# q and k with token parts side by side, layer norm's first steps a chunk later, and retention's output centred and gated before it is scaled

## The chip, the cores and the metric

The kernel runs on one core of a Trainium2 chip. A core has TensorE (matrix products, into PSUM), VectorE, ScalarE and GpSimd (elementwise work), and SyncE, whose queue issues the loads of the weights. Each engine runs its own list of instructions in order, and they are tied together by semaphores. The metric is the device time of one execution in microseconds (us), the median of a few runs.

## What is computed

The input is 256 tokens of 1024 channels in float32. A first block holds a gated delta rule layer and a short convolution layer; the change doesn't touch it. The second block is this:

```python
proj = h @ w_in                      # 256 x 1024 by 1024 x 11264
q, k, v, z_ret, u_val, u_gate, z_conv, g_a, g_b = jnp.split(proj, split_at, axis=-1)
qh, kh = rotary(q), rotary(k)        # 4 heads of 256 channels
ret = head_groupnorm(retention_chunkwise(qh, kh, vh))   # (o - mean) * rsqrt(var + eps), 4 heads of 512
y_a = (ret * silu(z_ret)) @ w_ret_out
a = u_val * sigmoid(u_gate)
a = causal_depthwise_conv_2(a, conv_w, conv_b)          # 31 taps over the tokens
a = silu(layernorm(a, conv_ln_g, conv_ln_b))
y_b = (a * silu(z_conv)) @ w_conv_out
merged = sigmoid(g_a) * y_a + sigmoid(g_b) * y_b
y = merged @ w_out                   # then norm, gate and residual
```

## The kernel before, in words

**Phases and chunks.** All products with weights are cut into chunks of 1 MB of weights, and the chunks into phases, in this order: qkv 16, z 8, gdn_out 8, sc_in 32, sc_out 8, glu 8, qk 8, v 8, zret 8, zconv 4, gates 8, ret_out 8, conv_out 4, w_out 4. There is no planner: the order of each engine is written out by hand, as a list of steps, one for each chunk, and what is put beside a chunk runs behind it on that engine.

**A product in three parts.** Every float32 factor is split into a high and a low part of the faster format float32r. A product is high by high, high by low and low by high. For the weights, ScalarE writes the high parts (`w_hi`, L1225) and VectorE the low ones (`w_lo = raw - w_hi`, L1795, helper `part_lo`), in halves of a chunk. In step j both make the second half of chunk j+1 and the first half of chunk j+2 (`split_hi`, `split_lo`), and then do what stands beside chunk j. `split_hi` waits until TensorE has finished the half that lay in the slot before (`half_done`), `split_lo` for `hi_ready`. TensorE waits for `hi_ready` ahead of the matmuls with `w_hi` of a half and for `lo_ready` ahead of those with `w_lo`. The load of a chunk into a ring of four slots `raw` waits for `lo_ready` of the chunk four before.

**Two forms of a chunk on TensorE.** `chunk` (L680, L681, L689) gives a half 16 matmuls of 256 columns with `w_hi`, by the high and by the low part of the tokens, and 8 with `w_lo`. `chunk_apart` (L698, L707) sends the high and the low part of the tokens, which lie side by side in `hT`, as one matmul of 512 columns, 8 for a half, and then the 8 of 256 with `w_lo`. The two parts' results then lie side by side in PSUM and must be added by someone: ScalarE copies one of them (`glu_part`), VectorE adds (`ug_sum`, `uv_sum`). sc_in and glu use `chunk_apart`, qk uses `chunk`. In a loop over a register, `chunk_apart` sends the matmuls with `w_hi` of both halves first and then those with `w_lo` of both. v, zret, gates, ret_out and conv_out go by `wide_half` (L730, L731, L737), where a half is 12 matmuls of 512 columns, those with `w_lo` last.

**VectorE beside the chunks.** The depthwise convolution is 8 channel blocks times 31 taps, 248 operations of 128x256 (`conv_op`, L2405 and L2408). `conv_share(n)` does the next n of them, and each step of glu, qk, v, zret, zconv and gates has its share. Beside qk, `rotate` multiplies a chunk in PSUM by cosine and sine (L2454, L2455) and writes `qkT` (L2457, L2458). `scores(c)` on TensorE (L1137) multiplies them behind the first four chunks of v; the first one waits for all rotations. Beside zret, TensorE does `weighted_sums` (retention's output o of head h and token tile t, in banks 4 to 7). VectorE takes its statistics (`bn_stats`, `bn_aggr` into `gmv`); ScalarE makes the square root (`grs`), VectorE the reciprocal and `gnm = -mean * grs`; ScalarE writes `og = o * grs + gnm` (L1676) from PSUM; and VectorE multiplies `og` by `zr` into `vt` (`gated`, L2490). Each head's work comes one head later; the last head's falls into zconv's first step. Behind each chunk of zconv, TensorE transposes a part of `vt` (`turn_two`, L1165), ScalarE and VectorE write it as `yT_hi`, `yT_lo` (`split_two`).

**Layer norm.** At the end of gates, VectorE adds up the convolution's channel blocks (`pair_sum`, `halves_sum`). Beside ret_out, TensorE sums over the channels by a product with ones behind chunk 1 (mean, L1174) and behind chunk 3 (variance, L1177). VectorE subtracts the mean, ScalarE squares (L1709), takes the root (L1712) and applies silu (L1716); VectorE makes the reciprocal (L2561), and the last piece is `cT_hi`, `cT_lo`, which conv_out reads.

Of the kernel before, what the change touches and what calls it, by code (L numbers as in the profile page):

```python
# [12 lines left out]
ALU = mybir.AluOpType  # L13
# [3 lines left out]
P = 128  # L17
# [82 lines left out]
def build(nc, x_in, pre_norm_w, post_norm_w, gdn_w_in, gdn_conv_w, gdn_A_log, gdn_dt_bias, gdn_norm_w, gdn_w_out,  # L100
# [3 lines left out]
    with ctx:  # L104
# [58 lines left out]
        gst, gmv, grs, gnm = new("gst", [P, NT, 6]), new("gmv", [P, NT, 2]), new("grs", [P, NT]), new("gnm", [P, NT])  # L163
# [73 lines left out]
        og = [at(f"og{t}", o_t + (9 + 2 * t) * K, [P, RDV]) for t in range(NT)]  # L237
# [344 lines left out]
        def _(pe):  # L582
# [241 lines left out]
            def wide_deep(name, a_hi, a_lo, operand, start=0, beside=None, between=None):  # L824

                g0 = FIRST[name]
                for c in range(start, COUNT[name]):
# [5 lines left out]
                    for h in range(2):  # L833
                        wide_half(g0 + c, h, c // 4 * 2, a_hi, a_lo, c % 4 * KH2, c % 4 == 0, c % 4 == 3, operand if c < 4 else None)
                    if beside is not None:
                        beside(c)

            def phase(name, a_hi, a_lo, beside=None, first=None, midway=None):
# [5 lines left out]
                def step(i):  # L844
                    for j in range(4):
# [5 lines left out]
                        elif name in ("sc_in", "glu"):  # L851
# [277 lines left out]
            def scores(c):  # L1129

                if c == 0:
                    pe.wait_ge(rp_step, 2 * RH)
# [81 lines left out]
        def _(act):  # L1214
# [425 lines left out]
            chunks("qk")  # L1640
# [25 lines left out]
            def group_norm(h):  # L1666
                act.wait_ge(gn_step, 2 * NT * (h + 1))
                if h:
                    act.wait_ge(gn_ready, NT * h)
                act.activation(grs[:, :], gmv[:, :, 1], ACT.Sqrt, bias=eps_n[:, :]).then_inc(gn_std, 1)  # L1670
                act.wait_ge(gn_rec, 2 * (h + 1))
                for t in range(NT):
                    n = NT * h + t
                    if h:
                        act.wait_ge(rg_ready, n - 1)
                    act.activation(og[t][:, :], psum[:, 4 + n % 4, :], ACT.Identity, scale=grs[:, t:t + 1], bias=gnm[:, t:t + 1]).then_inc(gn_ready, 1)  # L1676
# [26 lines left out]
            def layer_norm(i, j, done):  # L1703
                c = 4 * i + j
                if c == 1:
# [87 lines left out]
        def _(dve):  # L1793
# [622 lines left out]
            def glu_each(i, j, done):  # L2416
# [19 lines left out]
                if c >= 2:  # L2436
                    conv_share((3, 4, 5, 4, 2, 4)[c - 2])
# [12 lines left out]
            def rotate(i, j, done):  # L2450
                c = 4 * i + j
                conv_share(3)
# [210 lines left out]
```

## Time and profile before

| what | value |
|---|---|
| median of 3 runs | 835.33 us (835.25 to 835.35) |
| the profiled execution | 835.18 us |
| its span, first to last instruction | 833.4 us |
| TensorE busy | 826.0 us, 99% |
| VectorE busy | 731.4 us, 88% |
| ScalarE busy | 502.0 us, 60% |
| granted TensorE clock, mean | 0.999 |

The profile is of one execution; its time and the span differ by 1.8 us, which lie outside the first and last instruction. A busy time counts overlapping instructions of an engine once. TensorE's matmuls are pipelined: one is shown as 0.28 us (256 columns) or 0.39 us (512) long, while the next begins much sooner, so the distance of two starts is what one costs.

### The profile page before, as it was taken

Reading aid. Unit: us, or ns where it says so; the run is one execution under the profiler, and the core shown is the slowest. Engines: PE = TensorE matmul, PEld = TensorE weight load, DVE = VectorE, ACT = ScalarE, POOL = GpSimd, SP = SyncE. Lnnn points to the kernel's source line nnn. Section 1 sums busy time; section 2 is a strip of 40 time slices with the busy share of each in tenths; the row PEclk is TensorE's granted clock in tenths of the full one; section 3 lists DMA queues with packets and bytes.
Section 4 is the critical chain, followed back from the end, with each engine's and each line's share of the span. In section 5 each row is a group of like instructions: output and inputs, shape, how many; then the busy total and the mean of one; then the engine's idle time right before and its main releaser. Section 6 shows DMA issues by size and latency. Waiting matters only on the chain.

```text
span 833.4 us, 13964 instructions
## 1 busy us (share of the span) xinstructions
PE 826.0 (99%) x5158; PEld 727.3 (87%) x5158; DVE 731.4 (88%) x1195; ACT 502.0 (60%) x808; POOL 34.6 (4%) x38
## 2 busy tenths in 40 slices
PE   9999999999999999999999999999999999999997
PEld 8999998799888888888888788998888898888886
DVE  7799899868877888888979979999999998998774
ACT  6899858576566555555546675333456775546743
POOL 0001101241100000000000000000000001000000
PEclk9999999999999999999999999999999999999999
DMA  9875775601775777777775657555455446455531
GB/s 277 257 254 165 217 237 173 163 31 45 276 236 178 256 257 263 259 258 252 243 257 203 219 184 241 193 166 197 153 168 185 152 152 202 152 195 209 191 113 50
DMA packets 129882, 164.13 MB, mean 197 GB/s; under 512 B 17407, under 2 KB 92199, under 8 KB 129703
## 3 DMA queue, kind: packets, MB, share of 16 engines
q1 hardware_dynamic: 129831, 163.45, 59.8%
q8 instruction: 33, 0.54, 0.3%
q14 instruction: 18, 0.15, 0.1%
HBM read 159.20 MB, written 4.23 MB: 196 GB/s over the span
## 4 chain that ended last, share of the span: by engine, by line
PE 98%; DVE 1%; DMA 1%; issue 0%; ACT 0%; DVEq 0%; SPq 0%; ACTq 0%
PE psum L698 16%; PE psum L730 14%; PE psum L731 14%; PE psum L737 14%; PE psum L707 8%; PE psum L680 6%; PE psum L689 6%; PE psum L681 6%; PE psum L1031 2%; PE psum L634 1%; PE psum L644 1%; PE psum L638 1%; PE psum L1036 1%; PE psum L918 1%; PE psum L1137 1%; DMA x<-in_x_dram 1%
## 5 line engine op out<-in xcount | busy, mean ns | idle before, releaser
L1225 ACT ACTIVATE w_hi<-w_raw 128x1024 fp32r<-128x1024 f32 x255 | 266.5, 1061 | 182.8 <-PE psum L737 83.1
L1795 DVE TENSOR_TENSOR w_lo<-w_raw,w_hi 128x1024 fp32r<-128x1024 f32 x256 | 304.5, 1219 | 42.1 <-ACT w_hi L1225 40.0
L698 PE MATMUL psum<-hT,w_hi 128*128 128x512 f32 x576 | 138.9, 391 | 0.0
L698 PEld LDWEIGHTS psum<-hT,w_hi 128*128 128x128 f32 x576 | 105.4, 188 | 20.2
L730 PE MATMUL psum<-w_hi,hT 128*128 128x512 f32 x280 | 110.4, 394 | 0.0
L731 PE MATMUL psum<-w_hi,hT 128*128 128x512 f32 x280 | 109.2, 390 | 0.0
L680 PE MATMUL psum<-hT,w_hi 128*128 128x256 f32 x432 | 107.0, 285 | 0.0
L681 PE MATMUL psum<-hT,w_hi 128*128 128x256 f32 x432 | 105.9, 283 | 0.0
L2408 DVE SCALAR_TENSOR_TENSOR cv<-aP,par,cv 128x256 f32<-128x256 f32 x240 | 98.4, 476 | 0.0
L680 PEld LDWEIGHTS psum<-hT,w_hi 128*128 128x128 f32 x432 | 82.8, 192 | 0.2
L681 PEld LDWEIGHTS psum<-hT,w_hi 128*128 128x128 f32 x432 | 82.8, 192 | 0.1
L707 PEld LDWEIGHTS psum<-hT,w_lo 128*128 128x128 f32 x576 | 74.8, 191 | 3.3
L707 PE MATMUL psum<-hT,w_lo 128*128 128x256 f32 x576 | 76.1, 283 | 0.0
L730 PE MATMUL psum<-w_hi,yT_hi 128*128 128x512 f32 x192 | 75.9, 395 | 0.0
L737 PE MATMUL psum<-w_lo,hT 128*128 128x512 f32 x280 | 75.6, 389 | 0.0
L731 PE MATMUL psum<-w_hi,yT_lo 128*128 128x512 f32 x192 | 74.8, 390 | 0.0
L737 PEld LDWEIGHTS psum<-w_lo,hT 128*128 128x128 f32 x280 | 52.6, 188 | 11.1
L730 PEld LDWEIGHTS psum<-w_hi,hT 128*128 128x128 f32 x280 | 52.6, 188 | 10.5
L731 PEld LDWEIGHTS psum<-w_hi,hT 128*128 128x128 f32 x280 | 52.6, 188 | 10.5
L689 PE MATMUL psum<-hT,w_lo 128*128 128x256 f32 x432 | 60.6, 283 | 0.0
L689 PEld LDWEIGHTS psum<-hT,w_lo 128*128 128x128 f32 x432 | 55.7, 192 | 0.0
L737 PE MATMUL psum<-w_lo,yT_hi 128*128 128x512 f32 x192 | 52.7, 389 | 0.0
(346 smaller groups left out, 1114.9 us busy)
## 6 DMA issues: line engine op xcount, KB each, us to landing
w_raw<-in_w_in_dram SPq DMA_DIRECT2D x44, 1024.0 KB, 5.0
w_raw<-in_sc_w_in_dram SPq DMA_DIRECT2D x32, 1024.0 KB, 7.5
w_raw<-in_gdn_w_in_dram SPq DMA_DIRECT2D x23, 1024.0 KB, 7.2
ada<-in_w_ada_dram SPq DMA_DIRECT2D x24, 512.0 KB, 4.8
w_raw<-in_gdn_w_out_dram SPq DMA_DIRECT2D x8, 1024.0 KB, 5.6
w_raw<-in_sc_w_out_dram SPq DMA_DIRECT2D x8, 1024.0 KB, 5.6
w_raw<-in_w_ret_out_dram SPq DMA_DIRECT2D x8, 1024.0 KB, 5.1
w_raw<-in_w_conv_out_dram SPq DMA_DIRECT2D x4, 1024.0 KB, 5.0
```

The costliest lines, as they stand in the source:

```text
L680: pe.matmul(o[:, m, :], w_hi[s][:, k, mine], a_hi[:, ka, :], start=m == 0 and ka == 0, stop=False, skip_group_check=True)
L681: pe.matmul(o[:, m, :], w_hi[s][:, k, mine], a_lo[:, ka, :], start=False, stop=False, skip_group_check=True)
L689: mm = pe.matmul(o[:, m, :], w_lo[s][:, k, mine], a_hi[:, ka, :], start=False, stop=ka == KT - 1, skip_group_check=True)
L698: pe.matmul(o, w_hi[s][:, k, mine], hT[:, h * KH2 + k, :, :], start=h == 0 and k == 0, stop=False, skip_group_check=True)
L707: mm = pe.matmul(o, w_lo[s][:, k, mine], hT_hi[:, ka, :], start=False, stop=ka == KT - 1, skip_group_check=True)
L730: pe.matmul(psum[:, b + m, :], a_hi[:, ka, mine], wide(w_hi[s])[:, e, :], start=start and h == 0 and e == 0, stop=False, skip_group_check= ...
L731: pe.matmul(psum[:, b + m, :], a_lo[:, ka, mine], wide(w_hi[s])[:, e, :], start=False, stop=False, skip_group_check=True)
L737: mm = pe.matmul(psum[:, b + m, :], a_hi[:, k + 2 * h + e, mine], wide(w_lo[s])[:, e, :], start=False, stop=stop and h == 1 and e == 1, sk ...
L1031: mm = pe.matmul(b[:, a, :], left(a), right(a), start=True, stop=True)
L1225: act.activation((w_hi[half_slot(g, h)] if home is None else third_hi[half_slot(g, home)])[:, :, :], raw[slot][:, h * KH2:(h + 1) * KH2, : ...
L1795: return dve.tensor_tensor(o, whole, hi.bitcast(F32), ALU.subtract)
L2408: dve.scalar_tensor_tensor(out=cv[:, n, :], in0=src, scalar=w, in1=cv[:, n, :], op0=ALU.mult, op1=ALU.add).then_inc(cv_step, 1)
```

## The change

- qk's chunks take the form of `chunk_apart`. ScalarE copies the second half of the result (`beside_qk_2`), VectorE adds it to the first (`ug_sum`) and rotates from that sum.
- Retention's output: VectorE does `(o - mean) * zr` in one operation from PSUM into `vt`. ScalarE takes the square root for two heads at once and later multiplies four blocks of `vt` by the reciprocal deviation in place (`two_heads_std`, `two_heads_scaled`); VectorE makes one reciprocal for two heads. `gnm` and `og` are gone. `gn_ready` now counts VectorE's products, `rg_ready` ScalarE's scalings.
- Layer norm: the mean's product comes behind chunk 2 of ret_out, the variance's between the halves of chunk 4; the steps of ScalarE and VectorE that belonged to chunk 1 belong to chunk 2.
- The shares of the convolution: glu 3, 4, 6, 4, 3, 5 (25, was 22), qk 1 a chunk (8, was 24), the first step of gates 9 (was 4). The rest falls to the last step of gates.

```diff
-                        elif name in ("sc_in", "glu"):
+                        elif name in ("sc_in", "glu", "qk"):
                             chunk_apart(i, g0, j, midway if ahead and j == 2 else None)
...
-                if c == 1:
+                if c == 2:
                     pe.wait_ge(ln_sum_step, 4)
                     pe.matmul(psum[:, 6, 0:SEQ], ones, ln_sum[0][:, 0, :], start=True, stop=True).then_inc(mean_done, 1)
-                if c == 3:
+
+            def variance(c):
+                if c == 4:
                     pe.wait_ge(ln_sum_step, 8)
                     pe.matmul(psum[:, 7, 0:SEQ], ones, ln_sum[1][:, 0, :], start=True, stop=True).then_inc(var_done, 1)
-            wide_deep("ret_out", yT_hi, yT_lo, (y_op_ready, 2 * KT), beside=layer_norm)
+            wide_deep("ret_out", yT_hi, yT_lo, (y_op_ready, 2 * KT), beside=layer_norm, amid=variance)
...
-            chunks("qk")
+            def beside_qk_2(i, j, done):
+                c, g = 4 * i + j, FIRST["qk"]
+                act.wait_ge(half_done, done)
+                act.wait_ge(bank_free, 4 + g + c - 1)
+                act.activation(glu_part[j % 2][:, :, :], psum[:, 2 * j:2 * j + 2, SEQ:2 * SEQ], ACT.Copy).then_inc(sc_act, 1)
+            chunks("qk", beside_qk_2, unroll=True)
...
+            def two_heads_std(q):
+                both = slice(2 * NT * q, 2 * NT * (q + 1))
+                act.wait_ge(gn_step, 4 * NT * (q + 1))
+                act.activation(grs[:, both], gmv[:, both, 1], ACT.Sqrt, bias=eps_n[:, :]).then_inc(gn_std, 1)
+
+            def two_heads_scaled(q):
+                act.wait_ge(gn_rec, q + 1)
+                for n in range(2 * NT * q, 2 * NT * (q + 1)):
+                    h, t = n // NT, n % NT
+                    vh = slice(h * RDV, (h + 1) * RDV)
+                    act.wait_ge(gn_ready, n + 1)
+                    act.activation(vt[:, t, vh], vt[:, t, vh], ACT.Copy, scale=grs[:, n:n + 1]).then_inc(rg_ready, 1)
...
             def beside_zret(i, j, done):
                 c = 4 * i + j
-                if c and c % 2 == 0:
-                    group_norm(c // 2 - 1)
+                if c == RH:
+                    two_heads_std(0)
+                if c == RH + 2:
+                    two_heads_scaled(0)
                 z_ret(i, j, done)
...
             def turned_pairs(i, j, done):
                 if j == 0:
-                    group_norm(RH - 1)
+                    two_heads_std(1)
                 z_conv(i, j, done)
                 split_two(j)
+                if j == 0:
+                    two_heads_scaled(1)
...
-                    conv_share((3, 4, 5, 4, 2, 4)[c - 2])
+                    conv_share((3, 4, 6, 4, 3, 5)[c - 2])
...
             def rotate(i, j, done):
                 c = 4 * i + j
-                conv_share(3)
+                conv_share(1)
                 dve.wait_ge(half_done, done)
-                dve.tensor_tensor(rp1[:, :, :], bank(j), cos2, ALU.mult)
-                dve.tensor_tensor(rp2[:, :, :], bank(j), sin2, ALU.mult).then_inc(bank_free, 1)
+                dve.wait_ge(sc_act, 6 * KT - 2 + COUNT["glu"] - 2 + c + 1)
+                dve.tensor_tensor(ug_sum[:, :, :], psum[:, 2 * j:2 * j + 2, 0:SEQ], glu_part[j % 2][:, :, :], ALU.add).then_inc(bank_free, 1)
                 dve.wait_ge(bank_free, 4 + FIRST["qk"] + c + 1)
+                dve.tensor_tensor(rp1[:, :, :], ug_sum[:, :, :], cos2, ALU.mult)
+                dve.tensor_tensor(rp2[:, :, :], ug_sum[:, :, :], sin2, ALU.mult).then_inc(rp_step, 1)
...
+            def two_heads_inverse(q):
+                both = slice(2 * NT * q, 2 * NT * (q + 1))
+                dve.wait_ge(gn_std, q + 1)
+                dve.reciprocal(grs[:, both], grs[:, both]).then_inc(gn_rec, 1)
 
             def gated(h):
                 vh = slice(h * RDV, (h + 1) * RDV)
-                for t in range(NT):
-                    dve.wait_ge(gn_ready, NT * h + t + 1)
-                    dve.tensor_tensor(vt[:, t, vh], og[t][:, :], zr[:, t, vh], ALU.mult).then_inc(rg_ready, 1)
+                dve.wait_ge(gn_step, 2 * NT * (h + 1))
+                dve.wait_ge(bank_free, 4 + FIRST["zret"] + NT * (h + 1))
+                for n in range(NT * h, NT * (h + 1)):
+                    dve.scalar_tensor_tensor(out=vt[:, n % NT, vh], in0=psum[:, 4 + n % 4, :], scalar=gmv[:, n, 0:1], in1=zr[:, n % NT, vh], op0=ALU.subtract, op1=ALU.mult).then_inc(gn_ready, 1)
...
             def turned_pairs(i, j, done):
-                if j == 0:
-                    group_scale(RH - 1)
                 conv_share(5 if j else 8)
                 if j == 0:
                     gated(RH - 1)
+                    two_heads_inverse(1)
                 split_two(j)
...
-                conv_share(10 if c else 4)
+                conv_share(10 if c else 9)
```

## Rows read from the trace of the kernel before

**Rows 1.** The page's span and TensorE's busy time.
```profile
span 833.4 us, 13964 instructions
PE 826.0 (99%) x5158; PEld 727.3 (87%) x5158; DVE 731.4 (88%) x1195; ACT 502.0 (60%) x808; POOL 34.6 (4%) x38
```

**Rows 2.** What TensorE waited for from 470 us: us in total, times, longest.
```profile
PE psum L634 <- DVE hT L1985: 0.3, 1, 0.3
```

**Rows 3.** Timeline of TensorE: sc_in's chunks, qk's first matmul, v's first.
```profile
400.99 3.82 PE L698 MATMUL psum<-hT,w_hi 128*128 128x512 f32 x16
...
406.56 3.82 PE L698 MATMUL psum<-hT,w_hi 128*128 128x512 f32 x16
...
521.37 0.28 PE L680 MATMUL psum<-hT,w_hi 128*128 128x256 f32 x1
...
567.45 0.40 PE L730 MATMUL psum<-w_hi,hT 128*128 128x512 f32 x1
```

**Rows 4.** Timeline of VectorE, one chunk of qk and the next one's start.
```profile
531.01 2.36 DVE L1795 TENSOR_TENSOR w_lo<-w_raw,w_hi 128x1024 fp32r<-128x1024 f32 x2
533.29 1.27 DVE L2408 SCALAR_TENSOR_TENSOR cv<-aP,par,cv 128x256 f32<-128x256 f32 x3
534.48 0.68 DVE L2454 TENSOR_TENSOR rp<-psum,trig 128x512 f32<-128x512 f32 x1
...
535.79 0.43 DVE L2457 TENSOR_TENSOR qkT<-rp,rp 128x256 f32<-128x256 f32 x1
...
536.59 2.36 DVE L1795 TENSOR_TENSOR w_lo<-w_raw,w_hi 128x1024 fp32r<-128x1024 f32 x2
```

**Rows 5.** Timeline of VectorE and TensorE in v; idle time in brackets.
```profile
570.30 2.47 DVE L1795 TENSOR_TENSOR w_lo<-w_raw,w_hi 128x1024 fp32r<-128x1024 f32 x2
...
572.92 1.47 PE L1137 MATMUL psum<-qkT 128*128 128x256 f32 x8
...
591.95 1.23 DVE L1795 TENSOR_TENSOR w_lo<-w_raw,w_hi 128x1024 fp32r<-128x1024 f32 x1 [0.72 <-ACT w_hi L1225]
```

**Rows 6.** Timeline of VectorE in zconv's first step and the next one's start.
```profile
674.63 3.25 DVE L2408 SCALAR_TENSOR_TENSOR cv<-aP,par,cv 128x256 f32<-128x256 f32 x8
677.80 1.29 DVE L2490 TENSOR_TENSOR vt<-og,zr 128x512 f32<-128x512 f32 x2
679.00 1.28 DVE L1795 TENSOR_TENSOR yT_lo<-psum,yT_hi 128x512 fp32r<-128x512 f32 x2
680.20 2.49 DVE L1795 TENSOR_TENSOR w_lo<-w_raw,w_hi 128x1024 fp32r<-128x1024 f32 x2
```

**Rows 7.** Groups by line: count, busy us, mean ns, idle before and releaser.
```profile
L2254 DVE SCALAR_TENSOR_TENSOR yT_lo<-psum,nw_col,yT_hi 128x512 fp32r<-128x512 f32 x8 | 5.6, 745 | 1.6 <-ACT yT_hi L1568 1.6
...
L1709 ACT ACTIVATE a<-cv 128x512 f32<-128x512 f32 x4 | 2.4, 633 | 3.2 <-DVE cv L2552 3.2
```

**Rows 8.** Timeline of VectorE in gates: steps 0, 1, 2, 7 and ret_out's first.
```profile
698.71 1.23 DVE L1795 TENSOR_TENSOR w_lo<-w_raw,w_hi 128x1024 fp32r<-128x1024 f32 x1 [0.81 <-ACT w_hi L1225]
...
704.15 1.22 DVE L1795 TENSOR_TENSOR w_lo<-w_raw,w_hi 128x1024 fp32r<-128x1024 f32 x1 [1.50 <-ACT w_hi L1225]
...
709.11 2.35 DVE L1795 TENSOR_TENSOR w_lo<-w_raw,w_hi 128x1024 fp32r<-128x1024 f32 x2
...
740.26 2.35 DVE L1795 TENSOR_TENSOR w_lo<-w_raw,w_hi 128x1024 fp32r<-128x1024 f32 x2
...
744.50 1.22 DVE L1795 TENSOR_TENSOR w_lo<-w_raw,w_hi 128x1024 fp32r<-128x1024 f32 x1
```

**Rows 9.** Timeline of TensorE: ret_out's chunks 0 and 1, second half's `w_lo`.
```profile
742.69 1.07 PE L737 MATMUL psum<-w_lo,yT_hi 128*128 128x512 f32 x4
...
748.13 1.07 PE L737 MATMUL psum<-w_lo,yT_hi 128*128 128x512 f32 x4
```

**Rows 10.** Timeline of VectorE and TensorE where conv_out starts.
```profile
780.35 1.28 DVE L1795 TENSOR_TENSOR cT_lo<-cv,cT_hi 128x512 fp32r<-128x512 f32 x2
...
782.63 0.39 PE L730 MATMUL psum<-w_hi,cT_hi 128*128 128x512 f32 x1
```

More of the change, by code:

```diff
@@ L162, in build @@
         freq = new("freq", [P, 1])
-        gst, gmv, grs, gnm = new("gst", [P, NT, 6]), new("gmv", [P, NT, 2]), new("grs", [P, NT]), new("gnm", [P, NT])
+        gst, gmv, grs, gnm = new("gst", [P, NT, 6]), new("gmv", [P, NT * RH, 2]), new("grs", [P, NT * RH]), None
         xn = at("xn", o_ar, [P, NT, D])
@@ L236, in build @@
         cT_hi, cT_lo = at("cT_hi", o_ar, [P, KT, SEQ], F32R), at("cT_lo", o_q + 24 * K, [P, KT, SEQ], F32R)
-        og = [at(f"og{t}", o_t + (9 + 2 * t) * K, [P, RDV]) for t in range(NT)]
         zr = at("zr", o_yT, [P, NT, 2 * D])
@@ L822, in wide_blocks, with wide_deep @@
                             between()
-            def wide_deep(name, a_hi, a_lo, operand, start=0, beside=None, between=None):
+            def wide_deep(name, a_hi, a_lo, operand, start=0, beside=None, between=None, amid=None):
                 g0 = FIRST[name]
@@ L834, in wide_deep @@
                         wide_half(g0 + c, h, c // 4 * 2, a_hi, a_lo, c % 4 * KH2, c % 4 == 0, c % 4 == 3, operand if c < 4 else None)
+                        if h == 0 and amid is not None:
+                            amid(c)
                     if beside is not None:
@@ L2478, in _ @@
             chunks("v", decayed, unroll=True)
-            def group_scale(h):
-                dve.wait_ge(gn_std, h + 1)
-                dve.reciprocal(grs[:, :], grs[:, :]).then_inc(gn_rec, 1)
-                dve.wait_ge(gn_rec, 2 * h + 1)
-                dve.scalar_tensor_tensor(out=gnm[:, :], in0=gmv[:, :, 0], scalar=-1.0, in1=grs[:, :], op0=ALU.mult, op1=ALU.mult).then_inc(gn_rec, 1)
+            def two_heads_inverse(q):
+                both = slice(2 * NT * q, 2 * NT * (q + 1))
+                dve.wait_ge(gn_std, q + 1)
+                dve.reciprocal(grs[:, both], grs[:, both]).then_inc(gn_rec, 1)
             def gated(h):
                 vh = slice(h * RDV, (h + 1) * RDV)
-                for t in range(NT):
-                    dve.wait_ge(gn_ready, NT * h + t + 1)
-                    dve.tensor_tensor(vt[:, t, vh], og[t][:, :], zr[:, t, vh], ALU.mult).then_inc(rg_ready, 1)
+                dve.wait_ge(gn_step, 2 * NT * (h + 1))
+                dve.wait_ge(bank_free, 4 + FIRST["zret"] + NT * (h + 1))
+                for n in range(NT * h, NT * (h + 1)):
+                    dve.scalar_tensor_tensor(out=vt[:, n % NT, vh], in0=psum[:, 4 + n % 4, :], scalar=gmv[:, n, 0:1], in1=zr[:, n % NT, vh], op0=ALU.subtract, op1=ALU.mult).then_inc(gn_ready, 1)
             def group_norm(i, j, done):
@@ L2494, in group_norm @@
                 h, t = n // NT, n % NT
+                if n == RH + 1:
+                    two_heads_inverse(0)
+                conv_share(7)
                 if n and t == 0:
-                    group_scale(h - 1)
-                conv_share(7)
+                    gated(h - 1)
                 dve.wait_ge(ro_done, n + 1)
@@ L2500, in group_norm @@
                 dve.wait_ge(gn_step, 2 * n + 1)
-                if h:
-                    dve.wait_ge(gn_rec, 2 * h)
-                dve.bn_aggr(gmv[:, t, :], gst[:, t, :]).then_inc(gn_step, 1)
-                if n and t == 0:
-                    gated(h - 1)
+                dve.bn_aggr(gmv[:, n, :], gst[:, t, :]).then_inc(gn_step, 1)
             chunks("zret", group_norm, unroll=True)
             def turned_pairs(i, j, done):
-                if j == 0:
-                    group_scale(RH - 1)
                 conv_share(5 if j else 8)
```

19 lines of the change are left out of this document (5 added, 14 removed).

## The prediction

> **What bounds the kernel now.** I read the page first: TensorE is busy 99% of the span [rows 1], so a change pays only through TensorE: fewer of its columns or gaps, or a wait put into it. Next I asked for what TensorE waited in the second half. There is one wait of 0.3 us, ahead of the glu phase, and none behind it [rows 2]. So from qk to the end the time is the sum of TensorE's work; VectorE and ScalarE count only if a piece they deliver is late. Then I read the timelines of VectorE, ScalarE and TensorE side by side, to see how late each may be. The piece that matters is `w_lo`: VectorE makes two halves for each chunk of weights, and TensorE's last matmuls of a half (L737, L689, L707) wait for it.
>
> All times below are on the axis of the kernel before. What TensorE gains in qk moves everything behind it forward as a whole; I count lateness against TensorE.
>
> **qk on TensorE.** Before, a chunk is 48 matmuls of 256 columns, and the phase lasts from 521.37 to 567.45, 46.08 us [rows 3]. After, it is 16 matmuls of 512 and 16 of 256: as many columns, a third fewer instructions. sc_in has this form, in the same loop, at 406.56 - 400.99 = 5.57 us a chunk [rows 3]. Eight chunks: 44.56. Gain 1.52 us, and I take 1.50. This is all that TensorE can gain: the two small layer norm products only change places.
>
> The Trainium skill (TensorE: Matmul & The Clock Gate, Back-to-back issue gap) gives an isolated gap of N/2.4 + 2.5 ns, so that two matmuls of 256 for one of 512 would save 2.5 ns, and all 128 pairs of the phase 0.3 us. Its sustained figures would save much more. Neither is what sc_in's rows show, 1.5 us for the same 128 pairs; the rows decide.
>
> **qk on the other engines.** ScalarE gets 8 copies of a 128x512 half, about 0.6 us each; it idles far more than that in this phase. VectorE before, per chunk: two splits 533.29 - 531.01 = 2.28, three taps 1.19, two products 535.79 - 534.48 = 1.31 (0.60, and 0.71 where the next operation waits for the result), then 0.80 for the two halves of the rotation: 5.58 [rows 4]. After: 2.28, one tap 0.40, the sum of the two parts and the wait for it 0.71, products 1.31, rotation 0.80: 5.50, against 5.57 of TensorE. It just keeps up, but each step now starts when ScalarE's split of a chunk is there, late in TensorE's chunk. I put its last rotation at 4.7 us after the start of v (2.85 before: 570.30 against 567.45 [rows 3, 5]). `scores(0)` reads it 5.47 us after the start [rows 5], so 0.7 is left. In v VectorE is then 1.85 late; there it had 0.72 of idle time in its fourth step [rows 5] and a like piece two steps before, and what it does between the two is less than TensorE's chunk; that takes the 1.85 back to nothing by the middle of v. So on entering zret it stands as before.
>
> **zret.** ScalarE loses eight scalings from PSUM, and four of its table switches; its time here is free. VectorE, per head: gone are a reciprocal and the `gnm` product, together 0.28; the product with `zr` becomes one with a scalar out of PSUM. A pair of the old ones took 679.00 - 677.80 = 1.20 [rows 6]; the nearest row of the new form, L2254, averages 745 ns, and its eight, in pairs, take 5.6 us [rows 7], so 1.40 a pair, the last one's tail included, and 0.67 from start to start: 1.34, at most 1.49. Net about -0.13 a head, so VectorE is some 0.25 earlier at the end of zret. Bounds: -0.5 to +0.2.
>
> **zconv, where the new wait sits.** `two_heads_scaled(1)` stands in ScalarE's queue behind chunk 0, waiting for `gn_rec`, which VectorE gives behind eight taps (674.63, 3.17 us), `gated(3)` and a reciprocal [rows 6]: about 678.8. Then come four scalings. The nearest row, L1709's four SBUF operations of this shape, is 2.4 us [rows 7]; I take that, with 2.2 and 2.9 as the ends. Only at 681.25 may ScalarE start the split of zconv's chunk 2, second half, and behind it chunk 3's first. VectorE can take it up at 682.35; before it did so at 680.20 [rows 6]. TensorE does not see it (back from [rows 9] at its pace, it comes to that piece at about 686), but VectorE idles 2.1 us and carries them on: each later step of zconv is its own work back to back. At the first step of gates VectorE had 0.81 of idle time before 698.71 [rows 8], 0.9 counted from start to start; that much is absorbed, 1.15 stays.
>
> **gates.** Here the taps taken out of qk come back. Before gates VectorE has done 182 taps before and 169 after (glu +3, qk -16); so gates has 79 instead of 66: 9, then 10 in each of seven chunks, the last one included, where there were 2. The first gets five more, 1.98; idle time of 1.50 [rows 8] takes a good part. Chunk 2's step then starts at 709.11 + 1.15 + 0.40 = 710.66. Its steps are 6.23 each against TensorE's 5.44 (740.26 - 709.11 = 5 x 6.23), so nothing is caught up. Step 7 starts at 741.81 and its first split ends at 743.0: TensorE wants it at 742.69 [rows 9], the first stall, 0.5. Behind it: the second split (2.28 for both), ten taps 3.96, and 1.17 for the wait and the two sums (the old step's 744.50 - 740.26 = 4.24, less 2.28 and two taps); the next split starts at 749.2 instead of 744.50 [rows 8] and ends at 750.4. TensorE wants it at 748.13 [rows 9], and needs some 0.25 for wake-up and weights: 750.7. Stall in all 2.55 us, of which the first is a part.
>
> **The moved layer norm.** The mean one chunk later costs nothing: its sums end near 749.2, and the product stands behind chunk 2, at about 754.5. The variance moves half a chunk (2.7). Following ScalarE's splits, the square root and `inv`'s reciprocal, which have some idle time between them, I get 1.4 of it through to the first `cT_lo` (780.35 before, 0.68 long), which then ends at 782.4; conv_out starts at 782.63 and needs it about 0.25 sooner [rows 10]. I charge 0.15, bounds 0 and 1.3 (all of the 2.7 less the slack). DMA: a slot of `raw` is reloaded when its split is done, up to 2.5 us later in gates; the chunk is read some three steps after, so nothing.
>
> **The sum.** Profiled execution 835.18 us (span 833.4, 1.78 around it) - 1.50 + 2.55 + 0.15 = 836.38. The median of the runs is 0.15 above the profiled one: 836.5.
>
> What hides what: the 13 moved taps (5.15 us) lay under TensorE's work in qk at no cost, and would under gates if VectorE had room there; it has not, because gates is the one long phase where its steps exceed TensorE's.
>
> **Rivals.**
> 1. *The short stall.* ScalarE's scalings do not hold VectorE back (they start earlier, or zconv's slack takes all). Against it: the order of the queue. Then VectorE is only the 0.40 late from the first step, the stall is 750.7 - 1.15 - 748.13 = 1.4, and the time 835.2 to 835.3.
> 2. *No stall*, the whole gain: 835.33 - 1.50 = 833.8. It needs VectorE some 2.5 us earlier in gates than I have it. For it: the old slack there is 2.4 us (744.50 plus 1.22, against 748.13). Against: ten taps for two cost 3.2 alone.
> 3. *VectorE falls behind in qk too*, the case on the slow side. Place: the rotation, with a product of two waits more. Its step of 5.50 has 0.07 to spare. If it is 5.67, it is 0.8 us later at v: `scores(0)` stalls by 0.1, and as v's idle time is used up, the 0.8 goes through zret and zconv to gates and adds to the stall in full: 837.3. It decides from a step of 5.57 on. For it: only 0.07 of room; against: every part has a row.
> 4. *The wide matmuls gain little.* If two at 256 and one at 512 cost the same but for 2.5 ns, TensorE's qk gains 0.3, and all else stays: 835.33 - 0.3 + 2.7 = 837.7. sc_in's rows speak against it. It is the isolated-gap rule of the Trainium skill's page on TensorE named above.
>
> **How the numbers follow.** A measurement of this kernel can tell about 0.2%, 1.7 us, from no change: 833.66 to 837.0. Forecast 0.6; rival 1 0.15; rival 2 0.08; rival 3 0.14; rival 4 0.03. The forecast's own range is 835.7 to 837.3: 0.4 either way from ScalarE's four scalings, 0.3 from the scalar products, and the tail's 0.15 that may be nought. The range for 8 in 10 takes in rival 1 and part of 3: 834.8 to 837.5. Faster by over 0.2% would need more than the whole gain, or a gain in gates that I do not see: 0.05. Slower by over 0.2%: rivals 3 and 4 and the upper end of the forecast, 0.27. Within: 0.68.
>
> **What the profile after would show.** qk at 5.57 us a chunk on TensorE, no wait there. VectorE idle for about 2 us in zconv, waiting for `w_hi` of ScalarE; ScalarE four copies with scale in a row just before. In gates VectorE without idle time. Two waits of TensorE for `w_lo` of VectorE: near 0.5 us at ret_out's chunk 0, near 2 at chunk 1. None or a tenth at conv_out's start. Wrong would be: no wait of TensorE in ret_out (rival 2), one of about 1.4 only (rival 1), waits at L1137 or over 3 us in ret_out (rival 3).

## The result, and the profile after

| | before | after |
|---|---|---|
| median | 835.33 us (9 runs, 834.5 to 836.1) | 837.61 us (9 runs, 837.1 to 838.5) |
| the profiled execution | 835.18 us | 837.39 us |
| its span | 833.4 us | 835.4 us |

The ratio is 1.0028, with an interval of 1.0019 to 1.0037: slower, by 2.28 us. I had forecast 836.5 us, a range of 834.8 to 837.5, and "within 0.2%" as the likeliest case. The time is 0.11 us above the range and on the slow side of the bound for "slower" (837.0), though the interval's lower end touches that bound. 1.1 us were missing in the forecast.

The page of the kernel after, its span, its busy times and the chain that ended last:

```profile
span 835.4 us, 13706 instructions
...
PE 825.2 (99%) x5030; PEld 720.7 (86%) x5030; DVE 737.7 (88%) x1197; ACT 498.3 (60%) x810; POOL 36.4 (4%) x38
...
PE 76%; DVE 21%; ACT 1%; issue 1%; DMA 1%; DVEq 0%; SPq 0%; ACTq 0%
```

The same row of the chain in the kernel before:

```profile
PE 98%; DVE 1%; DMA 1%; issue 0%; ACT 0%; DVEq 0%; SPq 0%; ACTq 0%
```

TensorE has 128 matmuls fewer than in [rows 1] and still is busy 99% of the span. The sign of the trouble is in the chain: 21% of it runs over VectorE, where it was 1%. TensorE, though 99% busy, no longer sets the end alone.

What TensorE waited for from 400 us on, kernel after (us in total, times, longest):

```profile
PE psum L736 <- DVE w_lo L1809: 2.6, 3, 1.7
PE psum L633 <- DVE hT L1999: 0.3, 1, 0.3
```

The second row is the wait of [rows 2]; the first is new. Now TensorE's timeline in the kernel after: two chunks of qk, v's first `w_lo` and the first product of `scores`, then every piece with `w_lo` (one for each half of a chunk) from gates' last chunk to the first half of ret_out's chunk 2, and where ret_out ends and conv_out begins. The idle time ahead of a row stands in brackets.

```profile
521.32 3.82 PE L697 MATMUL psum<-hT,w_hi 128*128 128x512 f32 x16
...
526.88 3.81 PE L697 MATMUL psum<-hT,w_hi 128*128 128x512 f32 x16
...
567.69 1.07 PE L736 MATMUL psum<-w_lo,hT 128*128 128x512 f32 x4
...
571.32 1.47 PE L1138 MATMUL psum<-qkT 128*128 128x256 f32 x8
...
732.97 1.07 PE L736 MATMUL psum<-w_lo,hT 128*128 128x512 f32 x4
736.35 1.21 PE L736 MATMUL psum<-w_lo,hT 128*128 128x512 f32 x4 [0.50 <-DVE w_lo L1809]
739.24 1.07 PE L736 MATMUL psum<-w_lo,yT_hi 128*128 128x512 f32 x4
742.58 1.20 PE L736 MATMUL psum<-w_lo,yT_hi 128*128 128x512 f32 x4 [0.46 <-DVE w_lo L1809]
745.46 1.07 PE L736 MATMUL psum<-w_lo,yT_hi 128*128 128x512 f32 x4
749.99 1.19 PE L736 MATMUL psum<-w_lo,yT_hi 128*128 128x512 f32 x4 [1.66 <-DVE w_lo L1809]
752.85 1.07 PE L736 MATMUL psum<-w_lo,yT_hi 128*128 128x512 f32 x4
...
783.73 1.07 PE L736 MATMUL psum<-w_lo,yT_hi 128*128 128x512 f32 x4
786.49 1.07 PE L736 MATMUL psum<-w_lo,cT_hi 128*128 128x512 f32 x4
```

What the reader is to see: qk takes 5.56 us from one chunk to the next (5.57 over all eight), and at L1138, the place of L1137's 572.92 in [rows 5], TensorE is 1.60 us earlier. From there on it holds its lead until gates' last chunk. The piece at 749.99 is that of 748.13 in [rows 9], the second half of ret_out's chunk 1: 1.86 us later. So 3.46 us were lost between. The brackets give 2.62. A wait costs more than its bracket: undisturbed pieces are 2.72 us apart ([rows 9]: 5.44 for two), while 736.35 and 739.24 are 3.38 and 2.89 behind their forerunners, 0.83 us for a bracket of 0.50. The three waits cost 0.83, 0.78 and 1.95, of which 0.14 comes behind the piece at 749.99.

VectorE's timeline in the kernel after: a chunk of qk and the next one's start; zconv's second step; gates' steps 1 to 3 and 7, with ret_out's first.

```profile
526.19 2.36 DVE L1809 TENSOR_TENSOR w_lo<-w_raw,w_hi 128x1024 fp32r<-128x1024 f32 x2
528.46 0.48 DVE L2422 SCALAR_TENSOR_TENSOR cv<-aP,par,cv 128x256 f32<-128x256 f32 x1
528.86 0.69 DVE L2469 TENSOR_TENSOR ug_sum<-psum,glu_part 128x512 f32<-128x512 f32 x1
...
531.70 1.23 DVE L1809 TENSOR_TENSOR w_lo<-w_raw,w_hi 128x1024 fp32r<-128x1024 f32 x1
...
570.17 0.42 DVE L2475 TENSOR_TENSOR qkT<-rp,rp 128x256 f32<-128x256 f32 x1
...
680.60 2.61 DVE L1809 TENSOR_TENSOR w_lo<-w_raw,w_hi 128x1024 fp32r<-128x1024 f32 x2 [2.41 <-ACT w_hi L1228]
...
708.47 0.73 DVE L2419 TENSOR_SCALAR cv<-aP,par 128x256 f32<-128x256 f32 x2
709.12 2.36 DVE L1809 TENSOR_TENSOR w_lo<-w_raw,w_hi 128x1024 fp32r<-128x1024 f32 x2
711.38 5.08 DVE L2422 SCALAR_TENSOR_TENSOR cv<-aP,par,cv 128x256 f32<-128x256 f32 x10
716.39 2.35 DVE L1809 TENSOR_TENSOR w_lo<-w_raw,w_hi 128x1024 fp32r<-128x1024 f32 x2
718.66 4.04 DVE L2422 SCALAR_TENSOR_TENSOR cv<-aP,par,cv 128x256 f32<-128x256 f32 x10
...
741.32 2.34 DVE L1809 TENSOR_TENSOR w_lo<-w_raw,w_hi 128x1024 fp32r<-128x1024 f32 x2
743.59 4.03 DVE L2422 SCALAR_TENSOR_TENSOR cv<-aP,par,cv 128x256 f32<-128x256 f32 x10
...
748.72 5.76 DVE L1809 TENSOR_TENSOR w_lo<-w_raw,w_hi 128x1024 fp32r<-128x1024 f32 x5
```

Ten taps take 4.03 or 4.04 us in each of gates' last five steps; in the third step the same ten take 5.08. The group of those rows shows that one single tap has the excess (L2422 from 711.3 to 713.6 us: shortest, median and longest, in ns):

```profile
L2422 DVE SCALAR_TENSOR_TENSOR cv<-aP,par,cv x3: 472/472/1519, 711.4 to 713.2; 128x256 f32<-128x256 f32 x3
```

What lies beside it is GpSimd's second partial sum for the layer norm. GpSimd's timeline from 600 us on, first of the kernel after:

```profile
679.70 1.29 POOL L1800 TENSOR_TENSOR ln_sum<-cv 128x512 f32<-128x512 f32 x1 [458.47 <-ACT vt L1686]
708.70 3.92 POOL L1803 TENSOR_TENSOR ln_sum<-ln_sum,cv 128x512 f32<-128x512 f32 x1 [27.70 <-DVE cv L2422]
```

and its second sum in the kernel before:

```profile
701.65 2.14 POOL L1789 TENSOR_TENSOR ln_sum<-ln_sum,cv 128x512 f32<-128x512 f32 x1 [21.18 <-DVE cv L2408]
```

Before, this sum ended at 703.79, in VectorE's idle time that ends at 704.15 [rows 8]. It took 2.14 us there for the 1.3 that the first sum takes, so it was held up itself, but no operation of VectorE took longer for it. After, VectorE has no idle time in gates, and the sum becomes ready in the midst of VectorE's work. The trace suggests that GpSimd waited behind the two splits of 709.12 and then held up a tap for 1.05 us. That is close to the 1.1 us I lacked. Whether it is the cause, the experiments had to say.

### The profile page after: what moved, and what is told of

It is laid out like the page before. It is cut to its first block, busy times and chain, and to the rows that moved or that the text cites. A ratio compares the mean times of both kernels' runs of the same rounds, so it can differ in the third digit from the quotient of the medians.

```text
span 835.4 us, 13706 instructions
## 1 busy us (share of the span) xinstructions
PE 825.2 (99%) x5030; PEld 720.7 (86%) x5030; DVE 737.7 (88%) x1197; ACT 498.3 (60%) x810; POOL 36.4 (4%) x38
## 4 chain that ended last, share of the span: by engine, by line
PE 76%; DVE 21%; ACT 1%; issue 1%; DMA 1%; DVEq 0%; SPq 0%; ACTq 0%
PE psum L697 19%; PE psum L706 10%; DVE cv L2422 10%; PE psum L736 8%; PE psum L729 8%; PE psum L730 8%; DVE w_lo L1809 8%; PE psum L679 3%; PE psum L688 3%; PE psum L680 3%; PE psum L1032 2%; PE psum L633 1%; PE psum L643 1%; PE psum L637 1%; PE psum L1037 1%; PE psum L919 1%
## 5 line engine op out<-in xcount | busy, mean ns | idle before, releaser
L697 PE MATMUL psum<-hT,w_hi 128*128 128x512 f32 x704 | 169.5, 391 | 0.0
L697 PEld LDWEIGHTS psum<-hT,w_hi 128*128 128x128 f32 x704 | 129.0, 189 | 24.7
L2422 DVE SCALAR_TENSOR_TENSOR cv<-aP,par,cv 128x256 f32<-128x256 f32 x240 | 99.7, 484 | 0.0
L706 PEld LDWEIGHTS psum<-hT,w_lo 128*128 128x128 f32 x704 | 91.2, 191 | 3.9
L679 PE MATMUL psum<-hT,w_hi 128*128 128x256 f32 x304 | 75.6, 287 | 0.0
L680 PE MATMUL psum<-hT,w_hi 128*128 128x256 f32 x304 | 74.5, 283 | 0.0
L680 PEld LDWEIGHTS psum<-hT,w_hi 128*128 128x128 f32 x304 | 58.4, 192 | 0.1
L679 PEld LDWEIGHTS psum<-hT,w_hi 128*128 128x128 f32 x304 | 58.3, 192 | 0.2
L736 PEld LDWEIGHTS psum<-w_lo,yT_hi 128*128 128x128 f32 x192 | 35.9, 188 | 10.3 <-DVE w_lo L1809 3.0
```

The source lines that it names most:

```text
L679: pe.matmul(o[:, m, :], w_hi[s][:, k, mine], a_hi[:, ka, :], start=m == 0 and ka == 0, stop=False, skip_group_check=True)
L680: pe.matmul(o[:, m, :], w_hi[s][:, k, mine], a_lo[:, ka, :], start=False, stop=False, skip_group_check=True)
L697: pe.matmul(o, w_hi[s][:, k, mine], hT[:, h * KH2 + k, :, :], start=h == 0 and k == 0, stop=False, skip_group_check=True)
L706: mm = pe.matmul(o, w_lo[s][:, k, mine], hT_hi[:, ka, :], start=False, stop=ka == KT - 1, skip_group_check=True)
L736: mm = pe.matmul(psum[:, b + m, :], a_hi[:, k + 2 * h + e, mine], wide(w_lo[s])[:, e, :], start=False, stop=stop and h == 1 and e == 1, sk ...
L2422: dve.scalar_tensor_tensor(out=cv[:, n, :], in0=src, scalar=w, in1=cv[:, n, :], op0=ALU.mult, op1=ALU.add).then_inc(cv_step, 1)
```

## The experiments

**How they are compared.** The first 488 us are the same code in all kernels, and still varied by 0.7 us: the one `memset` of `aP` on VectorE, in glu, began at 487.65 in one run and at 488.34 in another. So I compare the tail, the span less the start of that instruction, and the lateness of one piece: TensorE's `w_lo` piece of ret_out that started at 748.13 in [rows 9], counted from the same `memset` and against the kernel before. e7 and e8 were timed in 11 runs each; the others have one run each, and for them the tail and the piece say more than the time. The spans are given to 0.1 us, so a tail can be off by 0.05. Where an expectation names a span, the late `memset` has to be taken off: e1 to e4 then have 834.5, 834.25, 833.4 and 835.8 for the 834.4, 834.2, 833.5 and 835.9 expected.

| kernel | span | `memset` | tail | tail against before | the piece |
|---|---|---|---|---|---|
| before | 833.4 | 487.71 | 345.7 | | |
| after | 835.4 | 487.66 | 347.75 | +2.05 | +1.91 |
| e1 GpSimd's second sum short | 834.5 | 487.65 | 346.85 | +1.15 | +0.98 |
| e2 scalings a step later | 834.8 | 488.21 | 346.6 | +0.9 | +0.73 |
| e9 both | 833.5 | 488.03 | 345.45 | -0.25 | -0.35 |
| e3 light last step | 834.1 | 488.34 | 345.75 | +0.05 | +0.05 |
| e4 taps and layer norm alone | 836.4 | 488.32 | 348.1 | +2.4 | +2.27 |
| e5 retention alone | 833.7 | 488.01 | 345.7 | 0 | -0.01 |
| e6 qk's form, old shares | 839.0 | 487.83 | 351.15 | +5.45 | +5.41 |
| e7 later and spread | 831.9 | 487.73 | 344.15 | -1.55 | -1.53 |
| e8 the same, old retention | 831.9 | 487.68 | 344.2 | -1.5 | -1.52 |

**e1: is it GpSimd's sum?** The kernel after, with GpSimd's second sum cut to 2 of 256 columns in each of its two blocks. The rest of that sum is left out, so the layer norm's mean is not the reference's; the data flow and every wait stay.

```diff
-            pool.tensor_tensor(ln_sum[0][:, :, :], ln_sum[0][:, :, :], cv[:, 4:6, :], ALU.add).then_inc(ln_sum_step, 1)
+            pool.tensor_tensor(ln_sum[0][:, :, 0:2], ln_sum[0][:, :, 0:2], cv[:, 4:6, 0:2], ALU.add).then_inc(ln_sum_step, 1)
```

> The kernel after, with GpSimd's second sum of the convolution's channel blocks cut from 512 columns to 2 a partition (so channel blocks 4 and 5 are left out of layer norm's mean, but for two tokens each). Theory (the 1.05 us that VectorE lost in gates beside that sum, 5.08 us for ten taps instead of 4.04, is passed on to TensorE in full): VectorE's ten taps take 4.04, TensorE's waits for w_lo at ret_out's chunk 1 and before are 1.05 shorter in sum, and the span is 834.4 instead of 835.4. Rival (VectorE's long step is hidden or comes from elsewhere, a weight load or the clock): the span stays at 835.4, or the ten taps stay at 5.1.

VectorE's ten taps in e1:

```profile
711.47 4.04 DVE L2422 SCALAR_TENSOR_TENSOR cv<-aP,par,cv 128x256 f32<-128x256 f32 x10
```

GpSimd's second sum in e1:

```profile
708.77 0.24 POOL L1803 TENSOR_TENSOR ln_sum<-ln_sum,cv 128x4 f32<-128x4 f32 x1 [27.71 <-DVE cv L2422]
```

TensorE's waits in ret_out in e1:

```profile
741.63 1.20 PE L736 MATMUL psum<-w_lo,yT_hi 128*128 128x512 f32 x4 [0.33 <-DVE w_lo L1809]
749.05 1.20 PE L736 MATMUL psum<-w_lo,yT_hi 128*128 128x512 f32 x4 [1.69 <-DVE w_lo L1809]
```

The ten taps take 4.04 again, and the tail is 0.9 us shorter. Nothing but GpSimd's sum was changed, so the collision is the cause of the 1.05, and it costs TensorE nearly all of that, 25 to 40 us later. What is left, +1.15, is what the prediction had summed up (+1.20), and its two waits stand where I had put them, at ret_out's chunks 0 and 1 (0.33 and 1.69 for "near 0.5" and "near 2").

**e2 and e9: the scalings' place, and whether the two delays add.** e2 is the kernel after with the second pair's four scalings one step later in ScalarE's queue; e9 has the edit of e1 as well (and leaves out the same part of the sum).

```diff
+                if j == 1:
+                    two_heads_scaled(1)
                 z_conv(i, j, done)
                 split_two(j)
-                if j == 0:
-                    two_heads_scaled(1)
```

> The kernel after, with ScalarE's second set of four scalings behind the splits of zconv's step 1 instead of in step 0. Theory (the scalings hold back ScalarE's split, VectorE waits 2.4 us for it and stays about 1.2 us late in gates): VectorE's wait in zconv goes, it stands at gates' first step some 1.2 earlier, and TensorE gets that back: span 834.2. Rival (what VectorE loses in zconv lies under its idle time at the start of gates, or the GpSimd sum takes it again): span 835.2 to 835.4.

> This is the kernel after with both suspected delays of VectorE ahead of gates treated at once: the four scalings of the second pair of heads stand one step later in ScalarE's queue, and GpSimd's second sum covers 2 columns of 256 (the rest of that sum is left out, so the layer norm's mean is not the reference's). The tail is the span less the start of VectorE's L2410 (347.75 us in the kernel after, 345.7 before). Theory (what delays VectorE reaches TensorE in full, and delays add up): the tail is 1.15 shorter by the first and 0.9 shorter by the second, 345.7 us; ten taps behind chunk 2's step of gates take 4.05 again; GpSimd's first sum still collides (five taps of 3.1 in zconv), and TensorE's one wait in ret_out is 0.7 to 1.1 us where the kernel with the later scalings alone has 1.68. Rival (one of the two hides the other, since TensorE waits for the later of two things): the tail stays at 346.6, as with the later scalings alone, or 346.85, as with the short sum alone.

e2's tail is 1.15 shorter than that of the kernel after. VectorE's wait of 2.41 in zconv is gone, and of TensorE's three waits one is left. But both of GpSimd's sums now meet VectorE. TensorE's wait in e2:

```profile
749.36 1.19 PE L736 MATMUL psum<-w_lo,yT_hi 128*128 128x512 f32 x4 [1.68 <-DVE w_lo L1809]
```

VectorE in e2, beside GpSimd's first sum and beside its second:

```profile
681.00 3.11 DVE L2422 SCALAR_TENSOR_TENSOR cv<-aP,par,cv 128x256 f32<-128x256 f32 x5
...
707.87 1.71 DVE L2419 TENSOR_SCALAR cv<-aP,par 128x256 f32<-128x256 f32 x2
```

Five taps take 3.11 where they took 2.06 beside nothing, and the two `TENSOR_SCALAR` 1.71 where they took 0.73. The first of these costs TensorE little: behind it VectorE still had idle time (0.38 us, ahead of the split at 697.73). In e9, with the second one gone as well, one wait of 1.06 stays on TensorE's timeline:

```profile
748.10 1.20 PE L736 MATMUL psum<-w_lo,yT_hi 128*128 128x512 f32 x4 [1.06 <-DVE w_lo L1809]
```

Its tail is 345.45 where 345.7 was expected for delays that add, and 346.6 or 346.85 if one hid the other. So neither hides the other: -1.15 and -0.9 alone, -2.3 together. That is 0.25 more than the sum of the two; no run here separates what the 0.25 is.

**e3: the last step's taps.** The kernel after with 2 taps in gates' last step, and 5, 3 and the layer norm's sums in ret_out's first two steps.

```diff
-                conv_share(10 if c else 9)
+                conv_share((9, 10, 10, 10, 10, 10, 10, 2)[c])
...
+            def layer_norm(i, j, done):
+                c = 4 * i + j
+                if c < 2:
+                    conv_share((5, 3)[c])
+                if c == 1:
+                    assert not conv_ops
                     dve.wait_ge(cv_step, CW * KT)
                     pair_sum(0, cv[:, KT - 2:KT, :], 2)
                     halves_sum(0, 3)
```

> The kernel after, with 2 taps instead of 10 in the last step of gates, 5 and 3 in ret_out's steps 0 and 1, and the two sums behind those. Theory (eight taps and the sums stand ahead of the split that ret_out's chunk 1 waits for): the third wait of TensorE, 1.66 us, goes and no other grows; the first two (0.50 and 0.46) stay; span 835.4 - 1.9 = 833.5. Rival (VectorE is late as such, and what is taken from this step is wanted in the next): a wait of over 0.5 us in ret_out's chunk 1 or 2 stays, span 834.5 or more.

The last and longest wait (1.66) is gone and the tail is 2.0 shorter. The first two stay, 0.49 at 736.98 and 0.50 at 743.21 us: VectorE is already late when the light step begins. So what stood in the last step, eight of its ten taps and the two sums, is about 2 us of the 3.46. The rest is what VectorE was late when that step began; the delays that e1 and e2 take away came in 25 to 60 us before the stalls.

**e4 and e5: the parts alone.** e4 is the kernel before with the new shares (shown here) and the layer norm's new places (as in the change above); qk and retention as before. e5 is the kernel before with retention's new order alone.

```diff
-                    conv_share((3, 4, 5, 4, 2, 4)[c - 2])
+                    conv_share((3, 4, 6, 4, 3, 5)[c - 2])
...
-                conv_share(3)
+                conv_share(1)
...
-                conv_share(10 if c else 4)
+                conv_share(10 if c else 9)
```

> The kernel before with only the shares of the convolution and the layer norm's places of the one after; qk and retention as before. Theory (the moved taps cost in gates, not qk's form): qk at 5.76 us a chunk as before, no wait in zconv, but in gates VectorE is 0.4 late from the first step, 1.05 from GpSimd's sum, and 3.2 at the last step; one or two waits of TensorE for w_lo, 2.5 us in all; span 833.4 + 2.5 = 835.9. Rival (the loss is in retention's new order alone): span 833.4, no wait.

Of e5's edit these are the main lines; the rest is the retention's part of the change as it stands above.

```diff
-                    dve.tensor_tensor(vt[:, t, vh], og[t][:, :], zr[:, t, vh], ALU.mult).then_inc(rg_ready, 1)
+                    dve.scalar_tensor_tensor(out=vt[:, n % NT, vh], in0=psum[:, 4 + n % 4, :], scalar=gmv[:, n, 0:1], in1=zr[:, n % NT, vh], op0=ALU.subtract, op1=ALU.mult).then_inc(gn_ready, 1)
```

> The kernel before with retention's new order alone (qk, the shares of the convolution and layer norm as before). Theory (the wait in zconv costs only through the taps in gates): VectorE waits about 2 us for w_hi in zconv and comes 1.1 late to gates, but with 4 taps in gates' first step its idle time of 1.50 in the second takes all of that; TensorE waits nowhere, and the span counted from the memset of aP stays at 345.7, as before, within 0.3. Rival (retention's order costs by itself): a wait of TensorE in ret_out, and 346.5 or more.

TensorE's one wait in ret_out in e4:

```profile
751.01 1.20 PE L737 MATMUL psum<-w_lo,yT_hi 128*128 128x512 f32 x4 [1.68 <-DVE w_lo L1799]
```

and the pair of VectorE's that meets GpSimd's sum in e4:

```profile
709.52 1.71 DVE L2409 TENSOR_SCALAR cv<-aP,par 128x256 f32<-128x256 f32 x2
```

The tail is +2.4 for the 2.5 expected: the taps alone lose more than qk's form gives. By my own steps it would have been 1.4 (the stall without the scalings' delay, as in rival 1), and the collision, 1.71 - 0.73 = 0.98, makes 2.4. So the collision belongs to the moved taps, not to retention. e5's tail is that of the kernel before, although VectorE's timeline has the same wait in zconv:

```profile
682.51 2.61 DVE L1799 TENSOR_TENSOR w_lo<-w_raw,w_hi 128x1024 fp32r<-128x1024 f32 x2 [2.41 <-ACT w_hi L1224]
```

With the old shares the idle time in gates takes it up. In the kernel after the same 2.41 costs the 1.15 that e2 gives back. One delay, free or not by what another edit left behind it.

**e6: were the taps moved for nothing?** The kernel before with qk's new form and the layer norm's places, but three taps a chunk in qk, and the other shares and retention, as before.

```diff
-                        elif name in ("sc_in", "glu"):
+                        elif name in ("sc_in", "glu", "qk"):
...
                 conv_share(3)
...
+                dve.tensor_tensor(ug_sum[:, :, :], psum[:, 2 * j:2 * j + 2, 0:SEQ], glu_part[j % 2][:, :, :], ALU.add).then_inc(bank_free, 1)
```

> The kernel before with qk's new form and layer norm's new places, but three taps in each chunk of qk as before, and retention as before. Theory (VectorE has no room in qk for more than one tap: its step is 6.3 us against 5.57 of TensorE): its last rotation is some 5.5 us later than in the kernel after, scores(0) makes TensorE wait 4 to 5 us, and the span counted from the memset of aP is 348.5 to 349.5 (before 345.7, after 347.7). Rival (qk's form itself was the gain, and the taps could have stayed where they were): 344.2, no wait.

VectorE in e6, the starts of two chunks' splits:

```profile
564.15 2.36 DVE L1805 TENSOR_TENSOR w_lo<-w_raw,w_hi 128x1024 fp32r<-128x1024 f32 x2
...
570.46 2.36 DVE L1805 TENSOR_TENSOR w_lo<-w_raw,w_hi 128x1024 fp32r<-128x1024 f32 x2
```

TensorE in e6, the first two products of `scores`:

```profile
576.79 2.92 PE L1139 MATMUL psum<-qkT 128*128 128x256 f32 x8 [3.83 <-DVE qkT L2471]
585.26 1.47 PE L1139 MATMUL psum<-qkT 128*128 128x256 f32 x8
```

Windows of 5 us in e6, busy times by engine and behind POOL's the granted clock (PEclk):

```profile
570.00:575.00 5.00, 2.42 (x10) 1.34 (x8) 4.93 (x9) 1.61 (x2) 0.00 (x0) 1.00 0.42 129
575.00:580.00 5.00, 3.21 (x10) 2.74 (x11) 4.93 (x9) 0.00 (x0) 0.00 (x0) 0.67 0.40 117
```

VectorE's step is 6.31 us against TensorE's 5.57; over seven chunks that makes some 5 us at the rotation that `scores(0)` reads. The tail is +5.45, where I had expected +2.8 to +3.8: a miss. The place was the expected one, the price was not. TensorE waits 3.83 us there, and 0.22 and 0.54 for two late `w_lo` ahead of it, 4.6 in all, in the expected 4 to 5. But the expectation had nothing for what came behind: the granted clock averaged 0.67 over 5 us, and the eight products took 2.92 us for 1.47, twice as long, as at the clock's lower level, 1.2 GHz. From this piece to the next of its line are 8.47 us, 6.80 in the kernel after (571.32 to 578.12); 1.67 us went that way. With the new form, taps had to leave qk; the question was only where to.

**e7 and e8: the mended versions.** e7 is the kernel after with e2's scalings and the taps spread evenly, the rest beside ret_out's first two steps. e8 has the same shares, with retention as in the kernel before. Each has 11 runs against 21 of the kernel before. Of e7's edit the new places of the taps and sums are shown; that of the scalings is e2's.

```diff
-                conv_share(10 if c else 9)
+                conv_share((9, 10, 9, 9, 9, 9, 9, 5)[c])
...
+            def layer_norm(i, j, done):
+                c = 4 * i + j
+                if c < 2:
+                    conv_share((5, 5)[c])
+                if c == 1:
+                    assert not conv_ops
                     dve.wait_ge(cv_step, CW * KT)
                     pair_sum(0, cv[:, KT - 2:KT, :], 2)
                     halves_sum(0, 3)
```

> The kernel after with both mends: the second set of scalings behind the splits of zconv's step 1, and the taps of gates as 9, 10, 9, 9, 9, 9, 9, 5, then 5 and 5 in ret_out's steps 0 and 1 and the two sums behind them. Theory (TensorE lost 1.6 us less than nothing in qk and all the rest in three waits for VectorE): no wait of TensorE for w_lo, the span from the memset of aP 344.2, time 1.4 us under the kernel before, about 834.0. Rival (the mends move the waits to another piece, or the two GpSimd sums take VectorE's room again): a wait of 0.3 us or more in gates or ret_out, 345 or more.

> As the run with both mends, but with retention's output as in the kernel before. Theory (retention's new order gives nothing, since neither ScalarE nor VectorE bounds there): no wait of TensorE for w_lo, 344.2 from the memset of aP, the same time as the run with both mends within 0.1%. Rival (the new order frees VectorE where it matters): 0.3 us or more longer than that run.

| | median | kernel before beside it | ratio | interval |
|---|---|---|---|---|
| e7 | 834.16 us | 835.46 us | 0.9986 | 0.9977 to 0.9995 |
| e8 | 833.82 us | 835.46 us | 0.9985 | 0.9976 to 0.9994 |

What TensorE waited for in e7 from 450 us on:

```profile
PE psum L633 <- DVE hT L1999: 0.3, 1, 0.3
```

TensorE's piece of ret_out in question, in e7:

```profile
746.62 1.07 PE L736 MATMUL psum<-w_lo,yT_hi 128*128 128x512 f32 x4
```

GpSimd's second sum in e7, and under it VectorE's nine taps beside it:

```profile
707.57 3.93 POOL L1803 TENSOR_TENSOR ln_sum<-ln_sum,cv 128x512 f32<-128x512 f32 x1 [25.85 <-DVE cv L2422]
```

```profile
710.26 4.70 DVE L2422 SCALAR_TENSOR_TENSOR cv<-aP,par,cv 128x256 f32<-128x256 f32 x9
```

The collision is there as before (nine taps 4.70, 3.65 in the other steps), and costs nothing, since VectorE is never late enough. The tail is 1.5 us shorter than before, qk's whole gain. Both are faster than the kernel before, by 0.14 and 0.15%. That is under the 0.2% I had set as the bound of what can be told, but here the intervals, from more runs, do not reach 1. e7 and e8 are alike in tail and piece: retention's new order adds nothing that the time shows. No run has the spread taps with the scalings in the place of the kernel after, so how much of e7's gain needs e2's edit is not measured.

## Why the prediction was wrong

The forecast's mechanism was found: qk gains, VectorE is late in gates, and TensorE waits for it in ret_out. What failed is one term, gates: it had VectorE's splits, taps and layer norm sums, and put GpSimd's sum, which runs beside them, at nothing. That sum cost VectorE 1.05 us, and TensorE 0.9 by e1.

- **qk, -1.50.** Held: 5.57 us a chunk, 1.60 us earlier at `scores`; e7's tail, free of stalls, is -1.55. VectorE's step is 5.51 (526.19 to 531.70), reckoned 5.50, and its last rotation ends at 570.59, 4.74 us after v's first matmul at 565.85; I had put it at 4.7. Nothing stalls there.
- **zret and zconv.** Held: a pair of the new products takes 1.40 us, as reckoned. ScalarE's split comes late and VectorE idles 2.41 us (reckoned 2.1). Its price, 1.15 of delay left over at gates, is what e2 gave back.
- **gates, the step that failed.** The third step was to start at 710.66 on the axis of before; it does at 709.12 + 1.60 = 710.72. From there I had "6.23 each". The third step took 7.27 (709.12 to 716.39). The four steps behind it take 6.23 each (716.39 to 741.32), and ret_out's first split starts at 748.72 + 1.60 = 750.32 where I had 749.2. By the 1.05 the first stall comes a chunk earlier than I had it, in gates' last chunk, and the stalls are 3.46 us in all for 2.55. e1 takes the collision away and gets +1.15 for my +1.20. The idle time of 1.50 in [rows 8] is the one into which that sum fell before; I spent it on taps and did not ask what else ran in it.
- **What was counted as a wait's price.** I had added 0.25 to a wait for wake-up and weights. The three cost 0.3 each beyond their brackets, so the allowance was about right, but is due once for each wait.
- **conv_out, +0.15.** Measured 0.04: ret_out's last piece is 2.00 later than before (783.73 for 781.73), conv_out's first 2.04 (786.49 for 784.45). The moved layer norm costs at most that.
- **The sum.** -1.55 + 3.5 + 0.04 = +2.0, the difference of the spans; the medians differ by 2.28, and the other 0.3 stays open. That the forecast came within 1.1 us owes 0.1 to luck: the charge for conv_out was not due and made up for a part of the collision.
- **The rivals.** The short stall (1) and no stall (2) are out: the scalings do hold VectorE up, and the stall is there. They came true only in e9 (a stall of 1.3, its tail's -0.25 + 1.55) and in e7. Rival 1's time was added up from the profiled execution; from the median, as the others, it is 835.4. VectorE behind in qk (3, 837.3) is out too: there is no wait at L1138 and the step is 5.51. So is the small gain of the wide matmuls (4), whose 837.7 is the number nearest to the measured one: they gain all that they should, and both numbers were near by chance. The isolated gap of the Trainium skill (TensorE: Matmul & The Clock Gate, Back-to-back issue gap) doesn't describe these chunks: by it all 128 pairs would save 0.3 us, and they saved 1.5 to 1.6.
- **The chances.** 0.27 for slower and 0.14 for a rival of that side were too low for a forecast 0.5 us from the bound with every delay passed on in full. What was left out of a full engine's list, as here, made it later, so the range should have reached further on the slow side.

## What to carry to other kernels

When work is moved into an engine's idle time, look at what the other engines do in this idle time. An operation there may have been free only because of the gap; once the gap is filled, the fuller engine carries the collision to the end of the phase. Where an engine's steps exceed those of the bounding engine and it has no idle time left, a delay is passed on, whatever its source (here 0.9 of 1.05 us); find the last place where there is slack and leave some of it there (here a share of 9 taps in place of 10, and the rest behind the phase). A busy share of 99% on the bounding engine doesn't show this; the chain, and the longest single instruction of a group, do.

## What the runs showed of the hardware

Where GpSimd's sums met taps or splits, the later one was held up for most of the other. One tap of 128x256 (two inputs in SBUF) took 1.52 us in place of 0.47 beside a GpSimd sum of 128x512, and this sum took 3.92 us in place of 1.29. With a `TENSOR_SCALAR` pair of VectorE, of one input each, it was 1.71 in place of 0.73, while the sum took 1.33. In six kernels (after, e2, e3, e4, e7 and e8) the second sum met taps or this pair, and VectorE lost 0.97 to 1.05 us, much the same whichever was hit. The first sum met five taps in e2, e7 and e9, which took 3.10 or 3.11 us for 2.06. In e5 it was a split, 1.98 us for 1.23, partly in idle time.

Not every operation was held up. In the kernel before, GpSimd's first sum runs beside VectorE's `yT_lo` pair, which reads PSUM and one SBUF tile and takes the usual 1.28 us [rows 6], and the sum takes its 1.30:

```profile
679.17 1.30 POOL L1786 TENSOR_TENSOR ln_sum<-cv 128x512 f32<-128x512 f32 x1 [458.31 <-DVE vt L2490]
```

The Trainium skill says this (SBUF — State Buffer, Who interferes with whom): VectorE's second port pair is GpSimd's too, an instruction of VectorE with two SBUF inputs contends with one of GpSimd that reads SBUF, and the second to issue "fully blocks". The traces agree for the taps: the excess of 1.05 us is most of the 1.3 us that the sum takes alone, and the `yT_lo` pair, with one SBUF input, lost nothing. For the operation with one input the page has the contention only in VectorE's modes with two ports; whether the pair ran in such a mode, no run here shows, but it was held up by 0.98 us.

The second thing is e6's clock: a wait of 3.83 us cost 1.67 us more behind it, as the granted clock fell (0.67 on average over 5 us) and the products ran at the lower level, while in the kernel after it stayed at 1.00 through the waits of up to 1.66 us.
